# Low halves of natural weight blocks made by a negated ScalarE copy and an adding DMA, in both MLP matrices of a two-layer trunk

## The reference

```python
def sq_relu_mlp(y, w_up, w_down):
    u = y @ w_up                      # 1024 x 4096
    return jnp.square(jax.nn.relu(u)) @ w_down   # 4096 x 1024

for i in range(DEPTH):                # DEPTH = 2
    ...
    h = h + y                         # the mixer's part
    h = h + sq_relu_mlp(rmsnorm(h, norm_gains[i, 1]), mlp_w_up[i], mlp_w_down[i])
h = rmsnorm(h, final_gain)
```

## Time and profile before

| | |
|---|---|
| median of 3 runs | 1192.46 us (1192.45 to 1192.54) |
| profiled execution, span | 1190.5 us |
| PE busy | 1177.8 us, 99% |
| DVE busy | 1012.5 us, 85% |
| ACT busy | 696.4 us, 58% |
| POOL busy | 114.4 us, 10% |
| mean granted TensorE clock | 0.997 of full |

### The profile page before, as it was taken

One profiled execution on the slowest core, in us unless ns is written; L12 is line 12 of the kernel. 1 busy time (PEld: TensorE's weight loads), 2 busy tenths in 40 slices (PEclk: granted clock), 3 DMA queues, 4 the chain that ended last, 5 costly groups with the idle time before them and its releaser, 6 DMA issues.

```text
span 1190.5 us, 22996 instructions
## 1 busy us (share of the span) xinstructions
PE 1177.8 (99%) x8809; PEld 1126.1 (95%) x8809; DVE 1012.5 (85%) x1623; ACT 696.4 (58%) x1201; POOL 114.4 (10%) x171
## 2 busy tenths in 40 slices
PE   9999999999999999999999999999999999999998
PEld 8999999999999999999999999987899988989988
DVE  6889888888889989998568988887898998999973
ACT  6777877745534544535357887876545355445453
POOL 3221110100110110101010000000001001001000
PEclk9999999999999999999999999999999999999999
DMA  7343342433463563673231212223336535546532
GB/s 179 95 113 85 89 109 77 146 110 106 109 143 106 116 136 107 148 208 111 57 104 54 68 57 78 80 69 119 100 132 126 132 118 113 124 124 143 162 106 72
DMA packets 152376, 131.89 MB, mean 111 GB/s; under 512 B 23208, under 2 KB 143072, under 8 KB 152288
## 3 DMA queue, kind: packets, MB, share of 16 engines
q1 hardware_dynamic: 141600, 104.93, 29.9%
q0 software_dynamic: 10560, 25.66, 10.9%
q10 hardware_dynamic: 128, 0.09, 0.0%
HBM read 111.43 MB, written 19.24 MB: 110 GB/s over the span
## 4 chain that ended last, share of the span: by engine, by line
PE 64%; issue 22%; DVE 8%; ACT 3%; DMA 1%; POOL 1%; SPq 0%; DVEq 0%; POOLq 0%; ACTq 0%
PE ps L2335 24%; PE ps L2027 18%; PE ps L2262 15%; PE ps L2553 2%; PE ps L2082 1%; DVE lo L1611 1%; ACT hi L741 1%; PE ps L2100 1%; DVE u L1662 1%; DVE tbuf L1662 1%; DVE lof L1604 1%; DMA h_sum<-abuf 1%; DVE tbuf L1667 1%; DVE lo L1618 1%; ACT ah L1029 1%
## 5 line engine op out<-in xcount | busy, mean ns | idle before, releaser
L741 ACT ACTIVATE hi<-lof 128x1024 fp32r<-128x1024 f32 x80 | 82.8, 1052 | 136.6 <-DVE lof L1604 136.6
L2027 PE MATMUL ps<-yh,wh 128*128 128x264 f32 (+1 forms) x704 | 160.5, 302 | 0.0
L2027 PE MATMUL ps<-yh,wl 128*128 128x264 f32 (+1 forms) x704 | 155.3, 295 | 0.0
L2027 PE MATMUL ps<-yl,wh 128*128 128x264 f32 (+1 forms) x704 | 155.3, 294 | 0.0
L2335 PE MATMUL ps<-th,hi 128*128 128x264 f32 (+1 forms) x448 | 127.0, 283 | 0.5 <-DVE tbuf L1662 0.5
L2335 PE MATMUL ps<-tl,hi 128*128 128x264 f32 (+1 forms) x448 | 126.4, 282 | 0.0
L2335 PE MATMUL ps<-th,lo 128*128 128x264 f32 (+1 forms) x448 | 126.3, 282 | 0.0
L2262 PE MATMUL ps<-ah,hi 128*128 128x264 f32 (+1 forms) x448 | 116.3, 318 | 0.3
L1611 DVE TENSOR_TENSOR lo<-lof,hi 128x1024 fp32r<-128x1024 f32 x80 | 97.1, 1222 | 22.1 <-ACT hi L741 20.5
L2262 PE MATMUL ps<-al,hi 128*128 128x264 f32 (+1 forms) x448 | 115.6, 316 | 0.0
L2262 PE MATMUL ps<-ah,lo 128*128 128x264 f32 (+1 forms) x448 | 115.4, 316 | 0.0
(11 more groups left out here) (332 smaller groups left out, 3370.6 us busy)
## 6 DMA issues: line engine op xcount, KB each, us to landing
raw<-in_mlp_w_up_dram SPq DMA_DIRECT2D x32, 1024.0 KB, 5.6
raw<-in_mlp_w_down_dram SPq DMA_DIRECT2D x32, 1024.0 KB, 5.0
raw<-in_diff_w_in_dram SPq DMA_DIRECT2D x24, 512.0 KB, 3.7
raw<-in_mlstm_w_in_dram SPq DMA_DIRECT2D x16, 512.0 KB, 5.3
h_sum<-abuf POOLq DMA_DIRECT2D x24, 264.0 KB, 4.8
h_sum<-abuf POOLq DMA_DIRECT2D x24, 256.0 KB, 5.2
h_sum<-h POOLq DMA_DIRECT2D x16, 264.0 KB, 2.4
h<-h_sum POOLq DMA_DIRECT2D x2, 2112.0 KB, 10.2
```

What stands on the lines that cost most here:

```text
L741: return nc.scalar.activation(o, i, ACT.Copy, scale=scale)
L2027: last = mm(ps[:, bank + s, 0:w_], w[:, slot, kb, :], m[:, kb, t0:t0 + w_], start=(kb == 0 and n == 0), stop=(kb == CB - 1 and n == 2))
```

## The change

For the natural blocks of crossed pairs DVE's subtraction goes away. ACT first copies the raw block times -1 into `lo` (rounded, so this is minus the high half), then makes the high half as before. POOL issues an adding DMA, raw added onto `lo` within SBUF, which leaves raw minus high. PE waits for that DMA (semaphores `nat_in`) in place of DVE's `m_lo`. The SP load of pair i+2 waits for both transfers of pair i, for its four forms and for its high halves, in place of `m_lo` alone. The raw tile is laid out in two column halves, so that A1 is one run of 4096 bytes in each partition, and each 1 MB load is now two DMAs of 512 KB in rows of 512 bytes. The adding DMAs stand in POOL's queue among the sends, in a fixed order.

```diff
@@ SP, mlp
-                        sp.wait_ge(m_lo, layer * N_READY + READY[i - 2, "A22" if crossed(i - 2) else 1])
+                        if by_dma(i - 2):
+                            for e in ("A1", "A22"):
+                                sp.wait_ge(nat_in[i % 2][e], nat_count(layer, i - 2, e))
+                            sp.wait_ge(s_made, 4 * (N_CROSSED * layer + RANK[i - 2]))
+                            sp.wait_ge(m_hi, layer * N_READY + READY[i - 2, "A22"])
+                        else:
+                            sp.wait_ge(m_lo, layer * N_LOW + LOW[i - 2, "A22" if crossed(i - 2) else 1])
...
-                    sp.dma_start(raw[:, i % 2, :, :], src).then_inc(m_raw[i % 2], 16)
+                    for s in range(2):
+                        sp.dma_start(raw[:, i % 2, s, :, :], half_of(src, s)).then_inc(m_raw[i % 2], 16)
@@ POOL, residuals
+                def low(i, e):
+
+                    rows, src = (slice(0, 8), raw[:, i % 2, 0, :, :]) if e == "A1" else (slice(24, 28), raw[:, i % 2, 1, second_k(i), :])
+                    pool.wait_ge(m_neg, N_SENT_LOW * layer + SENT_LOW[i, e])
+                    pool.dma_start(lo[1 - i % 2][:, rows, :].bitcast(F32), src, accum_op=ALU.add).then_inc(nat_in[i % 2][e], 16)
+
+                low(2, "A1")
+                for i in range(1, PAIRS):
+                    if sent_down(i - 1):
+                        send(i - 1, 1)
+                    if by_dma(i + 1):
+                        low(i + 1, "A22")
+                    if by_dma(i + 2):
+                        low(i + 2, "A1")
+                    if sent_down(i):
+                        send(i, 0)
                 pool.wait_ge(m_done, N_DONE * layer + DONE[PAIRS - 9, "A22"])
@@ ACT, natural_hi
+                    if by_dma(i):
+                        copy(lo[1 - i % 2][:, rows, :], src, -1.0).then_inc(m_neg, 1)
+                    copy(hi[1 - i % 2][:, rows, :], src).then_inc(m_hi, 1)
@@ DVE, natural_lo
+                    if by_dma(i):
+                        return
@@ PE, product
-                        pe.wait_ge(m_lo, ready + READY[i, group])
+                        if by_dma(i) and name in ("A11", "A22"):
+                            pe.wait_ge(nat_in[i % 2]["A1" if name == "A11" else "A22"], nat_count(layer, i, "A1" if name == "A11" else "A22"))
+                            pe.wait_ge(m_hi, layer * N_READY + READY[i, group])
+                        else:
+                            pe.wait_ge(m_lo, ready + LOW[i, group])
```

More of the change, by code:

```diff
@@ L110, with by_dma @@
 READY = counted((i, e) for i in range(PAIRS) for e in (("A1", "S23", "S14", "A22") if crossed(i) else (0, 1)))
+def by_dma(i):
+    return crossed(i)
+LOW = counted(x for x in READY if not (by_dma(x[0]) and x[1] in ("A1", "A22")))
+SENT_LOW = counted((i, e) for i in range(PAIRS) if by_dma(i) for e in ("A1", "A22"))
 PLAINS = counted((i, m) for i in range(PAIRS) if not crossed(i) for m in range(2))
@@ L255, in program @@
         wl = new("wl", [P, RING, CB, P], F32R)
-        raw = new("raw", [P, RAW, CB, 2 * P])
+        raw = new("raw", [P, RAW, 2, CB, P])
         tbuf = new("tbuf", [P, T])
@@ L409, in program @@
         half_in = sem("half_in")
+        nat_in = [{"A1": mrow_in[half], "A22": nrow_in[half]} for half in range(2)]
         qhi_done, qlo_done, khi_done, klo_done, v_t1, vt_rd1, meta_t, meta_rd = sems(
@@ L504, in square_out, with nat_count @@
             return halves(ab[m][:, t0:T])
+        def nat_count(layer, i, e):
+            return 16 * (HEADS // 2 - (e == "A1" and i % 2 == 0)) + 16 * sum(1 for _ in range(layer) for k in range(PAIRS) if by_dma(k) and k % 2 == i % 2) \
+                + 16 * sum(1 for k in range(i + 1) if by_dma(k) and k % 2 == i % 2)
         def sent_before(layer, i):
@@ L688, in residuals, with send @@
                 pool.wait_ge(h_saved, 16 * CB * (layer + 1))
[L689 to L696, removed]
-                        pool.dma_start(h_sum[2 * (i % 8) - 8 + m, :, t0:T], ab[m][:, t0:T], accum_op=ALU.add).then_inc(h_sent[m], 16)
+                def send(i, m):
+                    if crossed(i):
+                        pool.wait_ge(c_done, 7 * N_CROSSED * layer + summed(i, "C21" if m else "C12"))
+                    else:
+                        pool.wait_ge(m_evac, N_PLAIN * layer + PLAINS[i, m])
+                    pool.dma_start(h_sum[2 * (i % 8) - 8 + m, :, t0:T], ab[m][:, t0:T], accum_op=ALU.add).then_inc(h_sent[m], 16)
+                def low(i, e):
[12 more added lines that the diff above has]
+                        send(i, 0)
                 pool.wait_ge(m_done, N_DONE * layer + DONE[PAIRS - 9, "A22"])
@@ L747, in split @@
                     o = u - (U_OUT0, U_OUT1)[layer]
[L748 removed]
+                    act.wait_ge(raw_in[k // 2], 64 * layer + 32 + 32 * (o == 6) if k == 2 else 32 * layer + 32)
                 wait(act, unit_done, u - RING + 1)
[L751 removed]
+                copy(wh[:, k, :, :], raw[:, k // 2, k % 2, :, :]).then_inc(split_hi, 1)
             def split_unit(u, j, layer, head):
@@ L759, in split_unit @@
                 wait(act, unit_done, u - 2)
-                copy(wh[:, j, :, :], raw[:, j // 2, :, P * (j % 2):P * (j % 2) + P]).then_inc(split_hi, 1)
+                copy(wh[:, j, :, :], raw[:, j // 2, j % 2, :, :]).then_inc(split_hi, 1)
             def norm_prep(n, b, spans):
```

63 lines of the change are left out of this document (33 added, 30 removed).

## The result

The changed kernel takes 1212.48 us (median of 4 runs, 1209.22 to 1213.07) and the kernel before, on the same chip, 1192.45 (1191.95 to 1192.54). The ratio is 1.0161 [1.0149, 1.0173]: 20 us slower. The forecast was 1197 in a range of 1188 to 1211.

What follows compares the result with a forecast made beforehand. PE was taken as the bound, busy 1177.8 of 1190.5 us, with the sends' landing at group boundaries deciding. 1192.46 - 4.5 won + 5.7 of stalls + 3.4 of clock dips = 1197.1 us, forecast 1197, range 1188 to 1211.

Steps and rivals of the forecast that it cites:

- What can be won, 4.5 us: In the MLPs: 2.8 us of PE's waits on DVE plus 1.7 us of matmuls lost to a clock dip.
- rival A: Cheaper adding transfers: boundary stalls go and no new ones come, 1188.0 us, or 1189 with a rest; chance 0.28.
- DVE -69, ACT +60 us: Busy time: 80 subtractions leave DVE, 69 us; negated copies add 60 us to ACT; DVE's relief by itself worth nothing.
- What an adding transfer costs: Time on the 16 DMA engines: 3.0 us for low(i, A1) of 0.52 MB, 1.5 for low(i, A22) of 0.26 MB.
- rival B: Adding transfers as slow as the slowest sends, or slowed by 512-byte rows: 1223 or 1208 us; chance 0.22 together with D.
- The load of pair 16 "lands near 995": Ahead of the layer 1 boundary: the load in 512-byte rows is hidden, since ACT wants it at 996 or later.
- The burst of 15.7 us "to 1006.5": DMA work ahead of the layer 1 boundary, from 990.8: adding transfers, sends and pair 16's load, ending with send(14, 0).
- Stalls of the boundaries: PE at group boundaries: 1.2 us at each of three in layer 1, 0.7 at three in layer 0, 5.7 together.
- the clock dips: PE's clock falling after boundary stalls: two dips counted, 3.4 us.
- Read-back of h_sum "hidden": Late in the MLP: starts some 24 us later, at 545, lands at 553, wanted only after 559.42, so costs nothing.
- Rival D, the dependence through raw: Load-to-load chain outgrows two pairs' time: 1 to 2 us per each of eight groups, 1205; chance 0.22 with B.
- Copies, rows of 512 bytes, POOL's descriptors: Copies hidden except in down pairs' block forms (0.5 + 0.95 us); split loads hidden; descriptors only 0.85 us within each landing.

Runs made afterwards that it cites:

- e5_a1: The changed kernel with only A1's natural low halves by the adding transfer, A22's again subtracted by DVE: 1187.89 us, 0.9964 of the kernel before.
- e2_ups: The changed kernel with adding transfers only for the crossed up pairs: 1188.25 us, 0.9964 of the kernel before.
- e4_downs: The changed kernel with adding transfers only for the crossed down pairs: 1208.28 us, 1.0130 of the kernel before.
- e1_none: The changed kernel with only its layout and split loads; no negated copies or adding transfers, DVE subtracts as before: 1192.53 us, 1.0003 of the kernel before.
- e8_copies: e1_none plus ACT's negated copies, which DVE's own subtractions overwrite; no adding transfer: 1204.79 us, 1.0106 of the kernel before.
- e10_a22ups: The changed kernel without the A22 adding transfers of crossed down pairs, whose low halves DVE makes again: 1190.27 us, 0.9980 of the kernel before.
- e13_late: e5_a1 with the two loads behind crossed down pairs held until A1 of the pair before is negated: 1202.53 us, 1.0081 of the kernel before.
- e6_a22: The changed kernel with only A22's low halves by the adding transfer, A1's again subtracted by DVE: 1210.7 us, 1.0140 of the kernel before.
- e12_both: e10_a22ups with h_sum read back early, right behind the last send: 1197.78 us, 1.0042 of the kernel before.

## Why the prediction was wrong, point by point

The direction and the main place were right, the size was not: 20 us where 4.7 were forecast. By the prediction's steps:

- **What can be won, 4.5 us:** right. e5_a1 and e2_ups have no dip in the MLPs, and come out at 1187.9 and 1188.3 against rival A's 1188.0. They have rival A's outcome, but not its reason, which was a cheaper transfer.
- **DVE -69, ACT +60 us:** right to 6 us (-62.7, +63.5), and worth nothing, as said.
- **What an adding transfer costs:** right. The adding DMAs stand in queue 0, here before and after:

```profile
q0 software_dynamic: 10560, 25.66, 10.9%
```

```profile
q0 software_dynamic: 26688, 57.12, 24.8%
```

  0.248 x 1211.3 - 0.109 x 1190.5 = 170.6 us of 16 engines for 31.46 MB is 5.4 us/MB, where I had taken 3.0 us for 0.52 MB, 5.7. This is the time of packets that mostly had other traffic beside them, and takes the rest of queue 0 to cost what it did before. That is 2.2 times the 2.5 us/MB of the earlier trace rows. The Trainium skill (Collectives: The Full Stack, "The bandwidth ceiling") has an adding step at twice a copy, and the trace agrees within a tenth, with a read from HBM as the plain transfer. The Trainium skill's fit for one DMA (DMA: Bandwidth & Descriptors, "Anatomy of one DMA") doesn't hold for these: low(i, A1) landed after 6.8 us at the median and 4.6 at the least, not 3.2. So rival B's reason, dearer transfers, is out as well, though the time fell where B and D had it, above 1203.
- **The load of pair 16 "lands near 995": this is the step that failed.** It puts the landing 7.5 us into pair 14. It was issued even earlier than I had it (0.1 us into pair 14, forecast 1.25) and landed 12.0 us in, 9.7 to 12.0 at the six boundaries. low(15, A1) had been issued 0.4 us ahead of it, the two sends came 0.1 us behind, and the landing fits all of them sharing the engines. My own list of the burst, read one after the other (990.8 + 3.0 + 3.3 + 3.3 = 1000.4), gives 12.95 us. I had written the list for its total only, and then took the load's landing as if it went first.
- **The burst of 15.7 us "to 1006.5":** wrong for the same reason. It counts the work as back to back. But low(16, A1) can't be queued until the load has landed and ACT has negated it, 1.36 us more, and then it needs its own time to start; the engines were 12% busy from 1014 to 1016. low(16, A1) was issued 13.4 us into pair 14 and send(14, 0) landed 23.3 us in, where the forecast had 20.55. These 2.8 us are the 2.7 by which the stall there (3.93) missed the forecast of 1.2. 2.0 of them are the landing, 8.45 us after issue where the forecast had 6.4 (1001.6 to 1008.0). The other 0.7 is the issue, 14.9 us in for 14.15: the forecast put the wait of C11 for send(13, 0) at nothing, and it was 1.79 us. At the other five boundaries the issue was 1.0 us and more ahead of the forecast, and the landing alone was late.
- **Stalls of the boundaries:** forecast 5.7 us, measured 11.7. Hence **the clock dips:** forecast two, 3.4 us, measured six with 11.9, four of them at boundaries. That is 8.5 us of a miss of 15, and it isn't explained. In this trace 1.69 us brought no dip and 1.79 did, but the length of a stall doesn't decide it: in e4_downs three stalls of 2.27, 2.35 and 3.11 us have none, the last of them here with its window, and one of 1.89 has one.

```profile
1020.06 0.36 PE L2391 MATMUL ps<-yh,hi 128*128 128x256 f32 x1 [3.11 <-DVE abuf L1714]
```

```profile
1020.00:1022.00 2.00, 1.94 (x16) 1.97 (x17) 2.00 (x4) 0.00 (x0) 0.00 (x0) 1.00 0.18 31
```

  So counting dips by the size of the stalls was not a sound step, and a count of six is in part luck of the profiled execution.
- **Read-back of h_sum "hidden":** wrong in layer 1. Its own landing didn't matter; it slowed the load beside it, and `al` was late by 1.8 us with 1.7 of clock. A wait on low(17, A1) at 439.57, 2.12 us and a dip, was not foreseen either. It hangs on the load of pair 17, whose second half landed 11.1 us after its issue; where I had 2 us to spare in the up pairs, there were none behind this boundary.
- **Rival D, the dependence through raw:** its signs came, ACT's 77.8 us of waits on a load of `w_up` and PE's waits on the new transfers. Its reason is half right: the loads of pairs 16 and 17 do wait for a transfer of A22, but the length came from their landing, not from added steps. I had it at 1 to 2 us a group.
- **Copies, rows of 512 bytes, POOL's descriptors:** hidden in the change as far as e1_none, e5_a1 and e2_ups can tell; none of them has the A22 copies of the down pairs. e8_copies shows that the copies aren't free where DVE keeps its work.

The sum with the measured terms: 1192.5 - 2.8 + 11.7 + 2.3 + 1.8 of waits, and + 8.8 of slower PE, is 1214.3, 1.2 us over the profiled execution's 1213.07; the waits outside the MLPs aren't in it.

What is shown: that the twelve A22 transfers of crossed down pairs, with their copies and waits, make the loss (e10_a22ups), and that holding back the two loads behind each boundary makes a loss of the same kind without any added byte (e13_late). These five kernels put the load's lead over low(15, A1) beside what follows from it, in us and over all six boundaries:

| kernel | load ahead of low(15, A1) | its second half lands after | low(16, A1) issued, into pair 14 | send(14, 0) issued, into pair 14 | and lands after | median |
|---|---|---|---|---|---|---|
| e5_a1 | 1.9 to 3.9 | 5.4 to 9.1 | 8.7 to 9.1 | 13.3 to 14.1 | 5.4 to 6.7 | 1187.89 |
| e10_a22ups | 1.9 to 3.3 | 5.4 to 6.6 | 8.7 to 8.8 | 13.3 to 13.8 | 5.1 to 6.7 | 1190.27 |
| e13_late | 0.2 | 9.4 to 11.8 | 8.8 to 12.6 | 13.3 to 14.9 | 5.6 to 8.2 | 1202.53 |
| the change | -1.6 to -0.4 | 10.3 to 11.5 | 11.1 to 13.4 | 12.9 to 14.9 | 7.3 to 9.0 | 1212.48 |
| e4_downs | -2.1 to -0.4 | 10.3 to 11.8 | none | 14.6 to 18.7 | 3.9 to 5.2 | 1208.28 |

The lead goes with the landing, but isn't all of it: a lead of 2.0 us in e5_a1 came with 9.1 us once, and in e6_a22, which has no low(15, A1), the second half landed after 6.1 to 9.3 us.

What stays open: how the loss of the change splits between the boundaries and the end of the MLP, since the clock dips change from execution to execution; how much of the 22 us of e10_a22ups the twelve copies have beside the twelve transfers, since no kernel has one without the other there; and the 12 us of e8_copies.

The best kernel is e5_a1: A1 by the adding transfer, A22 by DVE, 0.36% faster than the kernel before and level with e2_ups.

## What to carry to other kernels

A list of what the DMA engines have to carry gives a total, and a landing only if nothing in it waits for something else in it: draw the order of arrival, and give each transfer the landing that its place in that order gives. Where a transfer is put into the path that frees a buffer, ask whether the next load still reaches the engines ahead of the traffic it used to lead; 2 us there were 6 us at the landing of the boundary shown, and 15 us over the kernel. And split such a change by operand and by place before judging it: here A1 alone gains 4 us, A22 alone loses 18, and A22 without that of the crossed down pairs some 2 us.

## What the runs showed of the hardware

- The second half of a 1 MB load landed 5.4 to 9.1 us after its issue when the load was issued 1.9 to 3.9 us ahead of an adding transfer of 512 KB and two sends (e5_a1, e10_a22ups), and 9.4 to 11.8 us after it when issued from 0.2 us ahead of such a transfer to 2.1 us behind it (e13_late, the change, e4_downs). The two halves split: in e13_late at the boundary shown the first landed after 4.3 us and the second after 11.8.
- Behind each of six stalls of 1.79 to 3.93 us in the change's trace the granted clock was at half, 1.2 GHz, long enough to cost 1.7 us, in one case 3.4. Behind 1.69 us in the same trace, and behind 2.27, 2.35 and 3.11 us in e4_downs, 1.88 in e13_late and 2.63 in e6_a22, it stayed at 1.00.
- A read of 2.16 MB from HBM into SBUF made a load beside it take 10.0 (the change), 11.0 (e6_a22), 13.9 or 15.3 us (both e12_both).
